# Hybrid decoder trunk in split fp32 on one core: the place of the last token chunk's transposes, and the loop order of the value groups

## The reference

```
for l in range(2):
    h = rmsnorm(x, norm_mix_pre[l])
    z = h @ w_in[l]                     # one projection, columns split over four mixers
    y = concat(short_conv(z_sc), conformer_conv(z_cf), moba_attention(z_moba), mla_attention(z_mla))
    x = x + rmsnorm(y @ w_out[l], norm_mix_post[l])
    f = conv_ffn_block(rmsnorm(x, norm_ffn_pre[l]), w_ffn_up[l], conv_ffn[l], w_ffn_down[l])
    x = x + rmsnorm(f, norm_ffn_post[l])
```

## Time and profile before

| | us |
|---|---|
| median of 3 runs | 1210.08 |
| lowest and highest | 1209.38, 1211.46 |
| the profiled execution | 1211.46 |
| its span, first to last instruction | 1209.7 |

### The profile page before, as it was taken

The page is one execution under the profiler, slowest core; times in us unless marked ns, Lnnn a source line. Parts: engine busy times, 40 slices in busy tenths (PEclk is TensorE's granted clock), DMA queues, the critical chain, the costliest instruction groups (busy, mean ns, idle before and its releaser), DMA issues.

```text
span 1209.7 us, 15326 instructions
## 1 busy us (share of the span) xinstructions
PE 1174.9 (97%) x6026; PEld 996.1 (82%) x6026; DVE 803.0 (66%) x1056; ACT 570.2 (47%) x861; POOL 205.8 (17%) x196
## 2 busy tenths in 40 slices
PE   6999989999999999999999999999999999999997
PEld 5887878798888888888898877888988888888886
DVE  5699765677666666544759887648766666664463
ACT  4455474554434343434445635745544344443432
POOL 1385173110000000000016833702000000000000
PEclk9999999999999999999999999999999999999999
DMA  8233332533333333566632333245323233336563
GB/s 250 75 88 85 92 78 95 184 98 114 102 90 105 91 101 94 168 194 212 199 103 80 88 92 94 87 135 157 94 87 105 88 105 95 96 100 200 176 226 134
DMA packets 155034, 146.83 MB, mean 121 GB/s; under 512 B 4783, under 2 KB 135763, under 8 KB 154963
## 3 DMA queue, kind: packets, MB, share of 16 engines
q1 hardware_dynamic: 154384, 145.12, 39.6%
q10 hardware_dynamic: 579, 0.74, 0.2%
HBM read 139.54 MB, written 2.10 MB: 117 GB/s over the span
## 4 chain that ended last, share of the span: by engine, by line
PE 79%; DVE 9%; ACT 3%; POOL 3%; issue 3%; DMA 2%; POOLq 0%; ACTq 0%; DVEq 0%
PE ps L555 25%; PE ps L557 25%; PE ps L556 25%; DVE wsp L457 2%; DMA raw<-in_w_out 2%; POOL rms_r L963 1%; POOL cf_out L972 1%; PE ps L849 1%; DVE ps L1258 1%; ACT wsp L449 1%; DVE yt L1058 1%; PE ps L617 1%; DMA rows<-in_vectors 1%; DVE xs L1071 1%; DVE x L1062 1%
## 5 line engine op out<-in xcount | busy, mean ns | idle before, releaser
L555 PE MATMUL ps<-xn,wsp 128*128 128x512 f32 (+1 forms) x1120 | 412.5, 368 | 3.0 <-DVE xn L1078 2.9
L556 PE MATMUL ps<-xn,wsp 128*128 128x512 f32 (+1 forms) x1120 | 409.3, 365 | 0.0
L557 PE MATMUL ps<-xn,wsp 128*128 128x512 f32 (+1 forms) x1120 | 409.3, 365 | 0.0
L457 DVE TENSOR_TENSOR wsp<-raw,wsp 128x1024 fp32r<-128x1024 f32 (+2 forms) x250 | 307.1, 1232 | 150.8 <-ACT wsp L449 150.6
L449 ACT ACTIVATE wsp<-raw 128x1024 fp32r<-128x1024 f32 (+2 forms) x256 | 265.7, 1041 | 159.0 <-PE ps L557 102.2
L555 PEld LDWEIGHTS ps<-xn,wsp 128*128 128x128 f32 x1120 | 211.9, 189 | 38.7 <-DVE xn L1078 4.1
L557 PEld LDWEIGHTS ps<-xn,wsp 128*128 128x128 f32 x1120 | 211.9, 189 | 33.9
L556 PEld LDWEIGHTS ps<-xn,wsp 128*128 128x128 f32 x1120 | 212.0, 189 | 33.6 <-issue 0.5
L555 PE MATMUL ps<-wsp,hid 128*128 128x512 f32 (+1 forms) x488 | 190.6, 391 | 0.8 <-DVE wsp L457 0.8
L557 PE MATMUL ps<-wsp,hid 128*128 128x512 f32 (+1 forms) x488 | 189.2, 388 | 0.0
L556 PE MATMUL ps<-wsp,hid 128*128 128x512 f32 (+1 forms) x488 | 189.1, 388 | 0.0
(11 more groups left out here) (157 smaller groups left out, 1226.7 us busy)
## 6 DMA issues: line engine op xcount, KB each, us to landing
raw<-in_w_ffn_up SPq DMA_DIRECT2D x88, 512.0 KB, 3.8
raw<-in_w_ffn_down SPq DMA_DIRECT2D x88, 512.0 KB, 4.1
raw<-in_w_in SPq DMA_DIRECT2D x36, 512.0 KB, 3.9
raw<-in_w_out SPq DMA_DIRECT2D x32, 512.0 KB, 3.6
x<-in_x SPq DMA_DIRECT2D x4, 512.0 KB, 8.1
xn<-xn SPq DMA_DIRECT2D x8, 256.0 KB, 3.3
out_x<-x SPq DMA_DIRECT2D x4, 512.0 KB, 4.0
raw<-in_w_vkr SPq DMA_DIRECT2D x4, 432.0 KB, 3.6
```

The lines of the kernel that those rows point to most:

```text
L457: eng.tensor_tensor(wsp[:, u % SPLIT, 1, 0:nk * n], raw[:, (l * NU + u) % RAW, 0:nk * n], fp(wsp[:, u % SPLIT, 0, 0:nk * n]), ALU.subtract ...
L555: pe.matmul(dst, a[0], b[0], start=start, stop=False, skip_group_check=True)
L556: pe.matmul(dst, a[0], b[1], start=False, stop=False, skip_group_check=True)
L557: return pe.matmul(dst, a[1], b[0], start=False, stop=stop, skip_group_check=True)
```

## The change

Two edits of TensorE's program. In `first_groups`, group j = 3 of half 0 is no longer cut in two: its 24 matmuls run in one piece, and the transposes of chunk 3 come behind them. In the value groups the loops are exchanged: the outer one goes over the two chunks, the inner one over all 8 k, with the wait for a weight unit at its first k; the wait for the bank of a chunk stands ahead of that chunk instead of ahead of both. The instructions are the same in number and shape, apart from a repeated wait on `vec_set` at n = 0 and repeated waits for the value units, on counts that were reached already.

```diff
--- before.py
+++ after.py
@@ -624,19 +624,13 @@
                     pe.wait_ge(xl_done, n * 2 * TC + 4 * half + 4)
                     for j in range(4):
                         weights_ready(l, u0 + j)
-                        rhs = [(a[:, cols], b[:, cols]) for a, b in x_pairs]
-                        if half == 0 and j == 3:
-                            dense(u0 + j, bank_of(g0 + j), rhs, cols=cols, ks=range(KD // 2))
-                            transposes_x(n, stage, 3)
-                            dense(u0 + j, bank_of(g0 + j), rhs, cols=cols, ks=range(KD // 2, KD))
-                            continue
-                        last = dense(u0 + j, bank_of(g0 + j), rhs, cols=cols)
+                        last = dense(u0 + j, bank_of(g0 + j), [(a[:, cols], b[:, cols]) for a, b in x_pairs], cols=cols)
                         if half:
                             last.then_inc(group_done, 1)
-                        elif j == 2:
+                        elif j >= 2:
                             if n == 0:
                                 pe.wait_ge(vec_set, DEPTH)
-                            transposes_x(n, stage, 2)
+                            transposes_x(n, stage, j)
 
             def chunk_product(u, k, nk, stage, c):
                 w = weights(u)
@@ -709,17 +703,15 @@
                 first_groups(l, 2 * l, FFN, 0, 0)
                 for g in range(4, G_MK):
                     if g in (G_V, G_V + 1):
-                        chunks = list(zip((2 * (g - G_V), 2 * (g - G_V) + 1), banks_of(g)))
-                        for _, bank in chunks:
+                        for c, bank in zip((2 * (g - G_V), 2 * (g - G_V) + 1), banks_of(g)):
                             bank_taken_over(l, g, bank)
-                        for k0 in range(0, KD, 3):
-                            weights_ready(l, U_VAL + k0 // 3)
-                            w = weights(U_VAL + k0 // 3)
-                            for c, bank in chunks:
-                                for k in range(k0, min(k0 + 3, KD)):
-                                    xk = [xn[:, k, s, c * P:(c + 1) * P] for s in range(2)]
-                                    last = product(ps[:, bank, 0:VKR], xk, (w[:, 0, k - k0, :], w[:, 1, k - k0, :]),
-                                                   k == 0, k == KD - 1)
+                            for k in range(KD):
+                                if k % 3 == 0:
+                                    weights_ready(l, U_VAL + k // 3)
+                                w = weights(U_VAL + k // 3)
+                                xk = [xn[:, k, s, c * P:(c + 1) * P] for s in range(2)]
+                                last = product(ps[:, bank, 0:VKR], xk,
+                                               (w[:, 0, k % 3, :], w[:, 1, k % 3, :]), k == 0, k == KD - 1)
                     elif g == G_KR:
                         bank_taken_over(l, g)
                         pe.wait_ge(kr_copied, l * 2 + 2)
```

## The result

The changed kernel took 1218.51 us (median, 1218.04 to 1219.19) against 1210.70 us: 7.8 us slower, ratio 1.0069 with a 95% interval of 1.0057 to 1.0081. The forecast was 1218.0 us. All 37 executions of it on record have a median of 1218.84 us (1217.09 to 1221.45); the profiled one, 1217.09 us, is the shortest.

A forecast was written before the change was run, and what follows sets the result against it. TensorE, busy 97% of the span, was taken as the bound, with no slack in the chain bringing `xn`. Transitions 5.7 us plus value groups 2.2 us made 7.9 us over the 1210.08 us median: 1218.0 us, range 1215.0 to 1222.0.

The forecast's parts named there:

- Part one: Four stage transitions: 12 matmuls put ahead of chunk 3's transposes delay TensorE's resumption by 1.43 us each, 5.7 us together.
- Part two: First value group of each layer: third weight unit wanted before VectorE's split lands, stalls plus restart bubbles, 2.2 us together.
- It comes through: Behind the value groups and transitions: other engines are released later too, so TensorE's next waits shift whole, nothing given back.
- a later wait that shrinks by what was lost: Sign that the forecast is wrong: a TensorE wait behind the edits gives the lost time back.
- The falling clock: Rival: clock falls to half behind the new transition pauses, 1.4 us per fall, 1219.5 to 1223.7 us; chance 0.17.
- the longest idle without a fall: TensorE's waits before the change: longest idle not followed by half clock, taken as 1.3 us.
- the transposes count as activity: Transition pauses: if transposes don't count as TensorE activity, the pause counts with its full 2.7 us, favouring a clock fall.
- Part two free: Rival at the value groups: VectorE gains during the pauses, third unit is in time, 1215.8 us; chance 0.08.
- transitions hidden: Rival at the transitions: moving the transposes costs nothing, only the value groups count, 1212.3 us; chance 0.04.
- faster: Rival: weight pipeline gets ahead during pauses and later waits vanish, measurably faster under 1207.7 us; chance 0.01.
- The rule on the pitch: Matmuls at the transitions: skill's warm pitch of 109 ns for 256 columns, making 12 matmuls 1.31 us, all transitions 5.2 us.

The follow-up runs named there:

- experiment 1: Kernel before with only the first edit (transposes of chunk 3 behind all 24 matmuls), value groups as before: 1216.82 us against 1210.48.
- experiment 5: Kernel before with the transposes of chunk 3 behind 6 of the 8 k of group j = 3 instead of 4: 1212.91 us against 1210.17.
- experiment 3: Changed kernel with VectorE splitting the third value unit one group earlier, behind the rotation of group 6: 1216.08 us against 1210.48 of the kernel before.
- experiment 4: Kernel before with only the second value group of each layer chunk by chunk: 1210.23 us against 1210.48.
- experiment 2: Kernel before with only the second edit (value groups chunk by chunk), transposes as before: 1212.82 us against 1210.48.
- experiment 9: Kernel before with three moves in ScalarE's and VectorE's queues ahead of the transitions, TensorE's program untouched: 1206.24 us against 1210.17.
- experiment 10: Kernel of experiment 9 with the transposes of chunk 3 behind 3 of the 8 k instead of 4: 1205.18 us against 1209.85 of the kernel before.
- experiment 6: Changed kernel with ScalarE making both copies of chunk 3 once more, lengthening the pauses: 17.7 us over the kernel before (1210.17 us).
- experiment 8: Changed kernel with ScalarE making only the second copy of chunk 3 once more: 12.9 us over the kernel before (1209.85 us).

## Why the prediction was right, point by point

**Part one, 5.7 us.** Right in place and size: 1.44 us in the stretch of the table, where 1.43 was summed. The chain from the first transpose to the resumption is 2.71 us in both orders. From one transition's resumption to what lies ahead of it the stamps grow by what was summed: 31.11 to 32.58 (1.47; the start of this profile is a little different, see below), and idle of 1.57 us in each of the four. Experiments 1 and 5 give the slope.

**Part two, 2.2 us.** Right: 1.02 us of stall against 1.03 worked out, and about 0.1 for the restart. Experiments 3 and 4 show that its cause is the split's place in VectorE's queue.

**It comes through.** Right. At the next wait in layer 0 (`rstd`), nothing was given back: the waits there and in attention are unchanged, and at the first row of `w_out` the changed kernel is behind by 208.90 - 206.35 = 2.55 us, where 1.43 + 1.13 = 2.56 were summed. That this difference fits to 0.01 us is partly luck, because the starts of these two profiles happened to agree. From the first dense matmul to the resumption at the first transition, the four profiles without an edit in that stretch take 15.12 us (before), 16.31, 16.12 and 15.14 (experiments 2, 4 and 9). It is the matmuls' pace that differs: between 15.9 and 19.3 us TensorE ran 20 matmuls in the kernel before and 16 in experiments 2 and 4 (29 in experiment 3). In the slower ones more of them start 0.21 us apart, as at half clock, although the profile gives a granted clock of 1.00 there for experiments 2 and 4. So a second part of the time, about 1 us and more, varies from run to run; behind it, 1.1 us of the second edit came through in experiment 2 as well.

**The `w_out` stage** had no place in the prediction: it left TensorE's 2.6 us of waiting for `xs` out of its rows, although that was the fifth longest wait. One of its signs of being wrong, a later wait that shrinks by what was lost, is seen in the two profiles for that reason (2.6 to 0.2 us). What they seem to give back there is variation. Between the same two instructions of layer 0, experiment 2 took 241.18 - 208.54 = 32.64 us and experiment 4, which costs nothing, 240.31 - 207.22 = 33.09 us, while experiment 1 took 239.20 - 207.52 = 31.68 us. The length doesn't follow the edits. Above the shortest, 31.7 us, stands the wait for `xs`. Three pieces of the chain that ended last, in the kernel before (start, length, what), then the same DMA in the changed kernel and, in layer 1, in experiment 1:

```profile
216.12 5.23 DMA raw<-in_w_out
221.51 0.83 issue
222.34 1.10 ACT junk L1441 x2
```

```profile
218.28 4.73 DMA raw<-in_w_out
```

```profile
812.29 6.08 DMA raw<-in_w_out
```

ScalarE's split waits for a DMA of `w_out`, and behind it in ScalarE's queue stands the square of `y` (`junk`) on which `xs` hangs. The traces tell that this DMA's landing is what varies. Counted from the stage's first wait (206.35, 208.90 and 802.54 us), it lands after 15.00, 14.11 and 15.83 us, and TensorE then waits 1.11, 0.22 and 1.94 us for `xs`: each time the landing less 13.9 us. The same holds for all 20 `w_out` stages of the ten profiles with this queue order, where the landing ranges from 13.4 to 16.2 us; where it comes before 13.9, the wait is 0.1 us. With the square put ahead, in experiments 9 and 10, it lands after 14.0 to 15.0 us, there is no wait, and all four stages take 30.97 to 30.99 us. Why the landing varies was not tried.

**The rivals.** The falling clock: not here (0 of 12 pauses), but near, as experiments 6 and 8 show; the 0.17 was not too much. One reading of this rival was off: the longest idle without a fall was not 1.3 us, as the earlier trace rows suggest, but the 1.5 us for `xs` that they leave out. Whether the transposes count as activity stays open: counted from them, the pauses are 2.71 us (no fall), 3.23 (experiment 8) and 3.86 (experiment 6), in the same order as the idle times. Part two free, transitions hidden, faster: against them stand experiments 2 and 3, 1 and 5, and the total.

**The rule on the pitch.** By the pitch of the Trainium skill ("TensorE: Matmul & The Clock Gate", section "Wait — 56ns, not 53.3ns?") part one would have been 5.2 us. The measured times can't tell 5.2 from 5.7. The rows of the changed kernel can: its pitch is 0.12 us, not 0.109, and the table has 1.44 us for 12 matmuls, not 1.31.

## What to carry to other kernels

Where an engine that bounds the kernel waits even 0.15 us for the end of a chain, that chain is the bound there, and here every matmul put ahead of its start was paid in full; look at where the chain starts, not at how long the wait is. A loop order decides when each weight is first wanted: before changing it, set the use of each unit against the end of its preparation in the other engine's queue. And before explaining a difference of two profiles, compare stretches that the change doesn't touch; here the two `w_out` stages differed by 2.3 us in the wrong direction, by a wait that had been left out of the list.

## What the runs showed of the hardware that had not been expected

TensorE's granted clock, behind a pause at a transition (8 transposes, then idle, with dense matmuls on both sides), was full in 12 of 12 cases at 1.57 us of idle, half in 4 of 4 at 2.09, half in 3 of 4 at 2.72 us, and half in 4 of 4 at 5.2. In a `w_out` stage it fell behind 1.9 and behind 2.3 us of idle. Half is 1.2 instead of 2.4 GHz, and cost 1.5 us each time, 2.0 to 2.2 behind the longest pauses. The same length of pause can thus go either way. A VectorE subtraction of 128x576 took 1.18 us in one place and 1.85 in another; GpSimd's additions ran beside both, so they alone don't tell the difference, and what lengthened it was not tried.
